# A two-block hybrid model on one core: rows of the split activations 2304 bytes long and operands at one place, single-tile loads, gates over four banks, output splits at other heads

## What is computed

```
for l in range(2):                                    # first block, two layers
    a, g, zc, q, k, v, za, qi, ki, wi = split(h @ w_in[l])
    y_conv = silu(layer_norm(conv31(a * sigmoid(g)))) * silu(zc)
    score  = sum_heads(relu(rope(qi) @ rope(ki)) * wi)         # causal
    y_attn = attention(rope(q), rope(k), v, keys = top132(score)) * silu(za)
    h = layer_norm(2**0.5 * h + concat(y_conv, y_attn) @ w_out[l])
# second block, one layer, 512 positions
q, k, v, ga, u, vin, gb, gm = split(rmsnorm(h) @ w_in_2)
ya = (attention(axial_rope(q), axial_rope(k), v) * silu(ga)) @ w_proj_attn
yb = (gelu(u) * (w_spatial @ layer_norm(gelu(vin))) * silu(gb)) @ w_proj_gmlp
out = rmsnorm(h + (sigmoid(gm0) * ya + sigmoid(gm1) * yb) @ w_out_2)
```

## Time and profile before

| | us |
|---|---|
| median of 3 runs (lowest, highest) | 1024.64 (1024.37, 1026.11) |
| the profiled execution, its own time | 1024.52 |
| its span | 1022.6 |
| TensorE busy | 987.3 (97%) |
| VectorE busy | 667.8 (65%) |
| ScalarE busy | 558.8 (55%) |
| GpSimd busy | 231.4 (23%) |

### The profile page before, as it was taken

The page is one execution under the profiler, slowest core; times in us unless marked ns, Lnnn a source line. Parts: engine busy times, 40 slices in busy tenths (PEclk is TensorE's granted clock), DMA queues, the critical chain, the costliest instruction groups (busy, mean ns, idle before and its releaser), DMA issues.

```text
span 1022.6 us, 15789 instructions
## 1 busy us (share of the span) xinstructions
PE 987.3 (97%) x6084; PEld 816.8 (80%) x6084; DVE 667.8 (65%) x1439; ACT 558.8 (55%) x915; POOL 231.4 (23%) x250
## 2 busy tenths in 40 slices
PE   7999999998999999999999999999999999999997
PEld 7888988886677988888778677888888788888886
DVE  3899999888674489999988756638422333333432
ACT  6685891645333558588165534544646566564442
POOL 0110771115211401077111512634101000000001
PEclk9999999999999999999999899999999999999999
DMA  8876874752001577488464400577777536365662
GB/s 301 196 180 179 210 181 131 166 124 83 1 1 50 157 177 176 124 185 187 124 171 79 156 21 1 171 180 188 176 210 197 114 89 158 90 158 126 175 155 82
DMA packets 23098, 143.92 MB, mean 141 GB/s; under 512 B 2785, under 2 KB 3297, under 8 KB 7281
## 3 DMA queue, kind: packets, MB, share of 16 engines
q0 software_dynamic: 8496, 60.36, 31.7%
q1 hardware_dynamic: 14528, 82.55, 22.8%
HBM read 140.81 MB, written 2.10 MB: 140 GB/s over the span
## 4 chain that ended last, share of the span: by engine, by line
PE 81%; ACT 7%; DVE 5%; DMA 3%; POOL 2%; issue 2%; SPq 0%; POOLq 0%; DVEq 0%; ACTq 0%
PE psum_B L1371 21%; PE psum_A L1371 14%; PE psum_B L1406 7%; PE psum_A L1406 7%; PE psum_A L1568 6%; PE psum_C L1448 3%; PE psum_A L1786 2%; PE psum_B L1568 2%; PE psum_B L1786 2%; PE psum_A L1484 2%; PE psum_B L1512 2%; DVE conv_acc L1887 2%; POOL w_lo L1155 2%; PE psum_B L1773 2%; PE psum_C L1371 1%
## 5 line engine op out<-in xcount | busy, mean ns | idle before, releaser
L1162 POOL DMA_DIRECT2D w_lo<-in_weights x59 | 52.0, 881 | 562.2 <-ACT w_lo L706 536.0
L1887 DVE SCALAR_TENSOR_TENSOR conv_acc<-u,vec,conv_acc 128x528 f32<-128x528 f32 (+1 forms) x240 | 172.3, 755 | 3.2
L1371 PE MATMUL psum_B<-x_hi,w_hi 128*128 128x264 f32 (+3 forms) x472 | 143.9, 338 | 2.5 <-DVE mlp_lo L2341 1.2
L1371 PE MATMUL psum_B<-x_lo,w_hi 128*128 128x264 f32 (+3 forms) x472 | 141.7, 333 | 0.0
L1371 PE MATMUL psum_B<-x_hi,w_lo 128*128 128x264 f32 (+3 forms) x472 | 141.2, 332 | 0.0
L705 ACT ACTIVATE w_hi<-w_raw 128x2048 fp32r<-128x2048 f32 (+2 forms) x73 | 113.4, 1553 | 18.7 <-DMA w_raw<-in_weights 18.2
L1371 PE MATMUL psum_A<-x_hi,w_hi 128*128 128x264 f32 (+3 forms) x408 | 111.1, 311 | 2.0 <-DVE za L2041 0.9
L706 ACT ACTIVATE w_lo<-w_raw 128x2048 fp32r<-128x2048 f32 (+2 forms) x73 | 112.7, 1544 | 0.0
L1371 PE MATMUL psum_A<-x_lo,w_hi 128*128 128x264 f32 (+3 forms) x408 | 109.1, 306 | 0.0
L1371 PE MATMUL psum_A<-x_hi,w_lo 128*128 128x264 f32 (+3 forms) x408 | 109.0, 305 | 0.0
L1371 PEld LDWEIGHTS psum_B<-x_hi,w_hi 128*128 128x128 f32 (+1 forms) x472 | 82.1, 186 | 13.4 <-issue 3.7
(11 more groups left out here) (407 smaller groups left out, 2199.5 us busy)
## 6 DMA issues: line engine op xcount, KB each, us to landing
w_raw<-in_weights SPq DMA_DIRECT2D x66, 1024.0 KB, 5.0
w_lo<-in_weights POOLq DMA_DIRECT2D x57, 1024.0 KB, 8.6
h<-in_x SPq DMA_DIRECT2D x1, 2048.0 KB, 11.0
out<-h SPq DMA_DIRECT2D x4, 512.0 KB, 2.6
x_first<-in_x_t SPq DMA_DIRECT2D x3, 528.0 KB, 8.3
post_ln_g<-in_post_ln_g SPq DMA_DIRECT2D x2, 512.0 KB, 4.7
post_ln_b<-in_post_ln_b SPq DMA_DIRECT2D x2, 512.0 KB, 6.1
w_raw<-in_weights SPq DMA_DIRECT2D x2, 288.0 KB, 6.4
```

What stands on the lines that cost most here:

```text
L1162: pool.dma_start(wlo[n % RING][:, 0:width], io["weights"][n, :, 0:width], accum_op=ALU.add) \
L1371: mm = pe.matmul(ps[0:cols, i, 0:b - a], w[wp][:, kt, at:at + cols], x[xp][:, kt, a:b], start=(kt == 0 and wp + xp == 0), stop=(kt == KD - ...
L1887: got = dve.scalar_tensor_tensor(dst, src, w, dst, ALU.mult, ALU.add)
```

## The change

Activations and places. `x_hi` and `x_lo` get rows of 576 elements, 2304 bytes, and are placed so that column 16 of every row is a whole number of 256 bytes away from byte 1152; small tensors move into the free 192 bytes behind the rows. `meta_pair` and the second block's tensors go to such places too. `h`, `ident`, `cos` and `sin` then stand 64 bytes short of one. The 528 columns go as pieces of 272 and 256 instead of 264 and 264, side by side across two banks, so ScalarE reads them as one run.

Loads. At the start x and the first weights are loaded and split in smaller pieces (8 of x, 5 of weights; before 5 and 3), and block 1 comes as two loads.

Order. The four small transposes of `index_weights` go into the middle of the product a of tile 2; ScalarE takes them before that product. `meta_values` writes bank C instead of the next of A and B, and the transposes of the convolution's gain and bias (`turn_affine`) follow it at once instead of at item 4. Gates take turns over banks A, B and C (the four ahead over A to D in layer 0, as before); their order is changed so that one block of gates is finished by item 7 in each layer (before by item 10). ScalarE does the weight splits of two items before what else is woven into them, and those of the output blocks come at earlier items. `conv_tanh` has one buffer instead of two. In the second block merge gate 1 goes behind two pairs of logits instead of ahead of them.

```
-FIRST_X = ((0, 1), (1, 2), (2, 4), (4, 6), (6, 8))
-FIRST_W = ((0, 2), (2, 4), (4, 8))
+FIRST_X = tuple((kt, kt + 1) for kt in range(KD))
+FIRST_W = ((0, 1), (1, 2), (2, 4), (4, 6), (6, 8))
+LINE = 256
+X_ROW = 576
+MIDDLE = END[2]
+HEAD = 512 - MIDDLE
 def column_halves(first):
-    mid = first + (L - first) // 2
-    return (first, mid), (mid, L)
+    return (first, MIDDLE), (MIDDLE, L)
...
-GATE_ITEMS = {0: (0, 1, 2, 3, 4, 5, 6, 7, 8, 10, 12, 14), 1: (0, 2, 4, 5, 6, 7, 8, 10, 12, 14)}
-GATE_BANKS = {0: "ABABABABAAAA", 1: "ABABABAAAA"}
+GATE_ITEMS = {0: (0, 1, 2, 3, 4, 5, 6, 7, 8, 9, 12, 14), 1: (0, 2, 4, 5, 6, 7, 8, 9, 12, 14)}
+GATE_BANKS = {0: "ABCDBCABACAA", 1: "CABCABACAA"}
 GATES_AT = {
     0: (("za", 2, 0), ("za", 3, 0), ("za", 2, 1), ("za", 3, 1),
-        ("zc", 0, 0), ("zc", 1, 0), ("zc", 2, 0), ("zc", 3, 0),
-        ("zc", 0, 1), ("zc", 1, 1), ("zc", 2, 1), ("zc", 3, 1)),
-    1: (("zc", 0, WHOLE), ("zc", 1, WHOLE), ("za", 2, 0), ("za", 3, 0), ("zc", 2, 0), ("zc", 3, 0),
-        ("za", 2, 1), ("za", 3, 1), ("zc", 2, 1), ("zc", 3, 1)),
+        ("zc", 0, 0), ("zc", 1, 0), ("zc", 0, 1), ("zc", 1, 1),
+        ("zc", 2, 0), ("zc", 3, 0), ("zc", 2, 1), ("zc", 3, 1)),
+    1: (("zc", 0, WHOLE), ("zc", 1, WHOLE), ("za", 2, 0), ("za", 3, 0), ("za", 2, 1), ("za", 3, 1),
+        ("zc", 2, 0), ("zc", 3, 0), ("zc", 2, 1), ("zc", 3, 1)),
...
 SPLITS_AT = {
-    0: ((0, 1, ("zc", 2)), (2, 3, ("wo", 0, 0)), (5, 6, ("wo", 1, 0)), (12, 13, ("wo", 0, 1)), (17, 19, ("wo", 1, 1))),
-    1: ((0, 1, ("zc", 2)), (2, 3, ("wo", 0, 0)), (7, 8, ("wo", 1, 0)), (12, 13, ("wo", 0, 1)), (17, 17, ("wo", 1, 1))),
+    0: ((0, 1, ("zc", 2)), (2, 3, ("wo", 0, 0)), (5, 6, ("wo", 1, 0)), (11, 13, ("wo", 0, 1)), (17, 19, ("wo", 1, 1))),
+    1: ((0, 1, ("zc", 2)), (2, 3, ("wo", 0, 0)), (5, 6, ("wo", 1, 0)), (9, 11, ("wo", 0, 1)), (17, 17, ("wo", 1, 1))),
...
-        xhi = sb("x_hi", [P, KD, L], F32R)
-        xlo = sb("x_lo", [P, KD, L], F32R)
+        X_AT = where[0] + LINE - 4 * META
+        xhi = sb("x_hi", [P, KD, X_ROW], F32R, at=X_AT)
+        xlo = sb("x_lo", [P, KD, X_ROW], F32R, at=X_AT + 4 * KD * X_ROW)
...
                     gates(i)
                     take_probs_t(l, i + 1)
+                    splits(i)
+                    splits(i + 1)
                     woven(i)
...
             def pieces_of(l, name):
                 if one_bank(l, name):
-                    return ((0, META, L),)
-                (a, m), (_, b) = column_halves(0)
-                return (0, a, m), (1, m, b)
+                    return ((0, 0, META, L),)
+                return (0, HEAD, 0, MIDDLE), (1, 0, MIDDLE, L)
...
-                    channels(l, name, c, buf=beside)
-                    if i == 0:
-                        index_weights(l)
+                    channels(l, name, c, beside, None if i else lambda: index_weights(l))
                     index_scores(l, 2 * i)
...
                 meta_values(l)
+                turn_affine(l)
...
-                if i:
+                if i > 2:
                     merge_gate(i // 2)
                 if i + 4 < n:
                     logits2(i + 4)
                     logits2(i + 5)
+                if i == 2:
+                    merge_gate(1)
```

More of the change, by code:

```diff
@@ L149, in gates_in_one_bank @@
         uses.extend((l, name, c, WHOLE) for name in ("za", "zc") for c in (0, 1))
-        uses.extend((l, name, c, half) for half in range(2) for name in ("za", "zc") for c in (2, 3))
+        uses.extend((l, name, c, half) for name in ("za", "zc") for half in range(2) for c in (2, 3))
     def gates(l, name):
@@ L154, in gates @@
             blocks.append(((l, name, c), BLOCK, (l, name, c + 1, 1)))
[L155 to L158, removed]
+        uses.extend((l, name, c + i, half) for c in (0, 2) for half in range(2) for i in range(2))
     for l in range(DEPTH):
@@ L416, in build, with small @@
         wlo = [sb(f"w_lo{i}", [P, BLOCK], F32R, at=RAW_AT + 4 * BLOCK * i) for i in range(RING)]
-        xhi = sb("x_hi", [P, KD, L], F32R)
-        xlo = sb("x_lo", [P, KD, L], F32R)
+        X_AT = where[0] + LINE - 4 * META
+        xhi = sb("x_hi", [P, KD, X_ROW], F32R, at=X_AT)
+        xlo = sb("x_lo", [P, KD, X_ROW], F32R, at=X_AT + 4 * KD * X_ROW)
+        where[0] = X_AT + 2 * 4 * KD * X_ROW
+        assert where[0] % 32 == 0 and (X_AT + 4 * META - 1152) % LINE == 0 and 4 * X_ROW % LINE == 0
+        spare = [X_AT + 4 * X_ROW * n + 4 * L for n in range(2 * KD)]
+        def small(n, *tensors):
+            made, at = [], spare[n]
+            for name, shape in tensors:
+                made.append(sb(name, shape, at=at))
+                size = 4
+                for d in shape[1:]:
+                    size *= d
+                at += -(-size // 32) * 32
+            assert at <= spare[n] + 4 * (X_ROW - L)
+            return made
         H_AT = where[0]
@@ L716, in full, with columns @@
                 return psum(use)
-            def halves(use, first):
-                n = (L - first) // 2
-                return full(use)[:, 0:2, 0:n], first
+            def columns(use):
+                return full(use).rearrange("p a n -> p (a n)")[:, HEAD:HEAD + L]
             def pair(ap):
@@ L741, in take_channels @@
                 first = META if wide else 0
-                ps = full(use)[:, 0, 0:SEQ] if wide else halves(use, 0)[0]
-                split = (lambda ap: ap) if wide else pair
+                ps = full(use)[:, 0, 0:SEQ] if wide else columns(use)
                 if name == "a":
@@ L1149, in _, with subtract_hi @@
         def _(pool):
-            def subtract_hi(n):
-                for half in range(2):
+            def subtract_hi(n, parts=(0, 1)):
+                for half in parts:
                     a, b = half * BLOCK // 2, (half + 1) * BLOCK // 2
@@ L1597, in term @@
                     def term(c, kt, wp, xp):
[L1598 to L1599 removed]
+                        for i, o, a, b in pieces:
+                            mm = pe.matmul(banks[c][0:cols, i, o:o + b - a], w[wp][:, kt, P * c:P * c + cols], x[xp][:, kt, a:b],
                                            start=(kt == 0 and wp + xp == 0), stop=(kt == KD - 1 and wp == 1))
```

131 lines of the change are left out of this document (69 added, 62 removed), and 2 rows, old and new, of the table OUTPUT_AT.

## The result

| | us |
|---|---|
| before, median of 4 runs (lowest, highest) | 1025.38 (1024.37, 1027.57) |
| after, median of 4 runs (lowest, highest) | 1017.88 (1017.43, 1019.36) |
| ratio, 95% interval | 0.9927 (0.9906 to 0.9947) |
| the profiled execution after, its span | 1017.43, 1015.6 |

The change gains 7.5 us, 0.7%. The sign was right; 17.1 us were forecast, and 1017.88 lies above the range of 1001 to 1017.

A forecast was written before the change was run, and what follows sets the result against it. TensorE, busy for 97% of the span, was taken as the bound, with VectorE limiting some stretches. Gains of 2.4 + 3.0 + 3.3 + 3.5 + 4.9 = 17.1 us took the median 1024.6 to 1007.5, range 1001 to 1017.

The forecast's parts named there:

- (6): Layer 1's items, to 642 us: gates 0.8, output rows 1.0, load and split order 1.7; together 3.5 us gained.
- the items give back: Rival, 13%: ScalarE's earlier splits wait for a load not yet there, exps behind them; 1014.4 us.
- (4): Layer 0's items: gates 0.8, output rows 1.0, order 1.2 with bounds -2 to +4; together 3.0 us gained.
- (1): Start: smaller load pieces let the first product begin sooner, worth 0; cost bounds 0 to +2 us.
- (3): Layer 0 up to item 0: TensorE gains 3.0 us, capped by VectorE's wait for exps at 2.4 us.
- (5): Layer 1 up to item 2: pairs, qi and q, gates ahead, index stage; 3.3 us gained, covered by VectorE's wait.
- (8): Second block: 4.0 us from matmul spacing, 0.9 from filling merge gate 1's wait; together 4.9 us gained.
- (7): From 642.05 to 666.40 us, a load, ScalarE, GpSimd subtractions and norms: nothing changed, 0.
- (2): Index weights: transposes moved into mid-product save 1.0 us per layer, no more, as VectorE is next.
- The place changes nothing: Rival, 12%: operand addresses have no effect; only index stage, items' order and merge gate gain 5.8 us, giving 1018.8.
- 64 bytes short costs nothing: Rival, 15% together with items' order at its upper bound: last product and layer 0 gates gain, 1004.9 or 1002 us.
- The loads and the moving reads collide: Rival, 5%: with all operands at one place each matmul goes slower by some 5 ns, giving 1033 us.

The follow-up runs named there:

- experiment 6: Changed kernel with layer 1's split of the second half block of output weights at items 12 and 13 instead of 9 and 11: 1014.42 us.
- 11: Changed kernel with channel products in pieces of 264 and 264 columns and layer 1's split at items 12 and 13: 1013.43 us.
- 10: Changed kernel with layer 1's split of that half block of output weights at items 12 and 14 instead of 9 and 11: 1014.69 us.
- 9: Changed kernel with layer 1's split of that half block of output weights at items 10 and 12 instead of 9 and 11: 1013.84 us.
- experiment 12: Changed kernel with pieces of 264 and 264 columns and layer 1's split at items 10 and 12: 1010.36 us, the fastest of the study.
- experiment 1: Separate kernel that only multiplies, runs of 48 matmuls per width and pair of places: 226.7 to 233.5 ns for 512 columns, 113.3 to 120.0 for 256.
- experiment 8: Changed kernel with the start of before, x in five pieces and first weights in three: 1017.54 us.
- experiment 5: Second multiply-only kernel with other places, narrower stationary operands and pairs of pieces: 512 columns at the place take 226.7 ns with 128 stationary columns, 231.6 with 32.

## Why the prediction was wrong, step by step

**The step that failed most: (6), the items of layer 1.** Forecast a gain of 3.5, measured a loss of 2.1. "The load waits for a gate, now at item 7 instead of 10, but the split comes at 9 instead of 12, so the distance shrinks too: I take 1.7 of it": the direction was wrong. I counted items, but did not put them on the clock. The load takes 10.6 us from the gate of item 7, the next split came 5.3 us after it, and ScalarE's queue holds exps behind. Since the splits of both items of a turn now stand together, the one of item 9 even comes ahead of item 8's own work. This is the rival "the items give back" (13%), with its mechanism as written: a split that waits for a load not yet there, exps behind it. With its -2 for the order this term would have been -0.2, and it had the same loss in (4), which was not there (a gain of 2.4). Part of the price is one that the rival did not have, matmuls at the lower clock behind the idle time. The wrong items cost 3.5 us of the whole (experiment 6). But 3.5 was also too much to ask: with the split elsewhere the stretch gains 0.3 and 0.5 (6, 11: items 12 and 13), 0.8 (10: 12 and 14), 1.8 and 2.6 (9, 12: 10 and 12). Part of what is missing at 12 and 13 is the norm beside GpSimd's subtraction, a wait for which the prediction has no term; the remainder stays open. The sign that the prediction named for being wrong, loads in the chain at items 8 to 12, is the line at 541.85.

**Second, the price of a column.** "0.4427 ns a column, and 6.7 more when either operand is off the place" holds for 512 columns with most places (226.7; 233.3 to 233.5 with the moving operand off by 32, 96, 128, 192 or 224 bytes), not with the moving operand 64 or the stationary one 192 bytes off (228.9, 229.0), and not for other widths. The two tests against pieces of 264 and 256 fitted within 0.8 ns because each mixed places: 117.5 ns for 256 columns is the mean of the four that rows of 2112 bytes give the stationary operand, 113.7, 118.7, 117.8 and 120.0 (experiment 1), and the place is the worst of them, not the best. The step that failed there is "a constant of 13 ns instead of a share would give 129 for 264 columns and is out": the 129 are 110 + 13.3 + 5.9, with the 5.9 for places carried over from 512 columns. Without them it is 123.3, for 122.3 read. So the pairs, forecast at -2.1 ns a matmul, came out at +1.0. In terms: the first row, (1) to (3), gained 1.5 instead of 2.4, VectorE's wait shrinking only to 1.07 us; (5) 1.6 instead of 3.3, of which 312 pairs at 246.6 instead of 240.4 ns are 1.9 us, and 2.4 to 2.5 with pieces of 264; `kv` lost 0.05 us a tile. The doubt stated with the earlier trace rows, kt 3 at 0.69 us instead of 0.68, stays unexplained by the table of experiment 1 too: it has 0.68 for kt 3, and over all four places a mean of 230.4 to 230.6 ns where the kernel before had 231.7.

**Right.** The 512-column products from column 16 came to 226.7, the merge gates to 228.4 (5.48 us for 24, forecast 5.44): over 16 gates that is 0.6 us of what (8) lacks. (8) gained 3.65 of 4.9: places 3.5 of 4.0, while moving merge gate 1 gave 0.1 instead of 0.9, since a wait of 0.78 us for its tanh came up behind it. The last product was better than forecast, 228.8 instead of 233.3: 64 bytes short costs 2.1 ns, not 6.7, in this direction. (1) was 0 (experiment 8), (7) was 0, (2) was 0.8 of 1.0 with VectorE's copy next, as said. (4) gained 2.4 of 3.0, within its bounds, though other traces of the same code have as little as 1.0.

Moving the split and taking back the pieces of 272 and 256, the answers to the first two points, brings the kernel to 1010.36 (experiment 12), 2.9 us from the 1007.5 forecast.

**The rivals.** "The place changes nothing" falls: undoing it costs 4.9 us. "64 bytes short costs nothing" is nearly right for the last product (2.1 ns of 6.7); for pieces of 272 columns no run has a moving operand 64 bytes short by itself. "The loads and the moving reads collide" had the right kind of mechanism, an effect of the two addresses on each other, the right sign for 256 columns (120.0 against 113.3) and the wrong one for 512.

What stays open is what lies behind the table of spacings. The Trainium skill says in "TensorE: Matmul & The Clock Gate", section "Step-by-step: what each phase is for", that the engine reads its two operands over two ports of their own and that a load takes no read bandwidth from the running matmul. That two addresses matter against each other, and hardly do so with a load of 32 columns (experiment 5), does not fit a plain reading of it. But with narrower loads the time for 512 columns at the place rose instead of falling, so what the load disturbs, and how, no run shows.

## What to carry to other kernels

Measure the spacing of back-to-back matmuls by itself, for each width and each pair of start addresses that the kernel uses, before rows are laid out: the best place for 512 columns (226.7 ns) was the dearest for 256 (120.0, against 113.3). Before a piece of work is moved ahead in a queue, write down when its data lands and when the queue gets there, in microseconds, and what stands behind it. And look for what a GpSimd subtraction lies beside: one VectorE instruction on the path with two SBUF inputs turned from 0.75 into 2.8 us.

## What the hardware showed that I had not expected

- Matmuls of 512 columns take 226.7 to 227.5 ns when both operands start at the same offset modulo 256 bytes, 228.9 or 233.3 when they differ by 64 bytes one way or the other; 256 columns take 120.0 at the same offset and 113.3 to 118.7 otherwise (120.0 with the moving operand 96 past). Below some 240 columns a matmul with a load of 128 columns takes 111.6 to 112.0 whatever its width (128 to 240 measured).
- 512 moving columns behind a load of 32 columns take 231.6 ns, behind one of 128 columns 226.7. With the load of 32 the stationary operand's place no longer counts (231.6 and 231.7), with 128 it does (226.7 and 233.3).
- A VectorE instruction with two SBUF inputs that met a GpSimd subtraction ended 0.55 us after it, in each of four cases: norms of 1.75, 1.77, 2.82 and 2.83 us instead of 0.75.
- Behind 2.7 and 2.3 us between the starts of two matmuls (552 to 558 us) the next 24 matmuls took 4.88 us instead of 3.07. By their starts the second to the 19th stand 213.4 ns apart and the last five about 119; at 517.87 six spacings of 512 columns are 427 and, from the ninth on, 226 to 232. So at the lower level, 1.2 GHz, the spacing is columns / 1.2 (213.3 and 426.7), without the 13 ns that 512 columns show at the place over columns / 2.4.
